# Recurrence channels in 11 tiles of five groups, and K's rope summed by VectorE

## The chip, the cores and the metric

One core of a Trainium2 chip runs the whole program. The metric is the device time of one execution in microseconds (us), here the median of three runs; a profiled execution stands beside them.

## The reference, cut to what matters

Two transformer blocks follow each other on x of 256 tokens by 1024 channels, all in fp32. The first has a gated linear recurrence over 1344 channels beside three forms of attention, and a feed-forward part. The second has attention with rope beside a gated mixing unit, and another feed-forward part. The change touches the recurrence of the first and the rope of the second.

```python
def rg_lru(x, w_a, b_a, w_x, b_x, lam):          # 16 blocks of 84 channels
    xb = x.reshape(bsz, s, RNN_BLOCKS, RNN_BLOCK_W)
    r = sigmoid(einsum('bsnc,ncd->bsnd', xb, w_a).reshape(...) + b_a)
    i = sigmoid(einsum('bsnc,ncd->bsnd', xb, w_x).reshape(...) + b_x)
    log_a = LRU_C * r * log_sigmoid(lam)
    a = exp(log_a)
    u = sqrt(-expm1(2.0 * log_a)) * (i * x)
    ...                                          # h[t] = a[t] * h[t-1] + u[t]
hr = rg_lru(causal_dwconv(rx, rnn_conv_w, rnn_conv_b), ...)
y_rnn = (hr * gelu(rgate)) @ w_rnn_out           # 1344 -> 1024

def rope(t, pos):                                # q and k of the second block
    rot = concatenate([-t2, t1], axis=-1)
    return t * cos + rot * sin
```

## The kernel before, in words

All weights come as one stream, cut into chunks of up to 128 x 2048 fp32 (1 MB), in the order of the list `chunk_list()`. For a split chunk ScalarE makes a rounded first part WH (L577), and VectorE the rest WL = RAW - WH (L965); TensorE multiplies both, three matmuls of 256 tokens for each 128 x 128 of weights (`f_tile`, L1576 to L1578) or of 512 columns (`t_part`, L1600 to L1602). Raw weights have two slots, split ones three. All waits are on semaphores, and the order on each engine is written out by hand: each engine runs one loop over the chunks c. TensorE does the scores of one attention unit (`unit_qk`, L1639 and L1643), the chunk's own matmuls (`main`), and `window`. ScalarE and VectorE do in it the split for chunk c + 2, their part of the unit, `side(c)` (what reads this chunk's result) and `window`.

The part around the change has 24 chunks, counted w = 0 to 23 from `W0`. The 1344 channels are 16 blocks of 84. Four blocks make a group of three tiles of 126 rows, so there are 12 tiles in four groups of equal size (RG = 3, NG = 4). A group is three rnn chunks (a tile of rx and of rgate each), an mg chunk (gates of the merge), the gate chunk ri and another mg chunk, so the gate chunks are w = 4, 10, 16 and 22. Tiles 0 and 1 of a group share the fourth block, half each. Its crossing parts are extra matmuls on 42 rows (L1859, L1861), added to the banks of tiles 0 and 1. Tile 2 has none. It is therefore computed and read first (`GATE_ORDER = (2, 0, 1)`), and its semaphore `ri_part` is counted at once:

```python
for m, t in enumerate(GATE_ORDER):          # ScalarE, side() of an ri chunk
    bank = wait_mb(eng, c, m)
    ...                                     # tanh to TR and TI, L729 and L730
    if m == 0 and i:
        rg_first(i - 1)
    if m == 0 and 0 <= c - W0 - 3 < NU:
        unit_exp(c - W0 - 3)
```

The rest of a group's work is placed by steps counted from its gate chunk: logarithm (`rg_log_a`) one chunk on, exponential and square in that chunk's `window`, a product on VectorE two on, square root and gelu (L650, L652, ScalarE) three on, the product with the input (`rg_input`) four on, the scan over the tokens with the product by the gelu (`rg_scan`, L1027 and L1029) five on, and the two parts for ro (`rg_first`, L603, and `rg_second`, L1033) six on, in the next gate chunk. The last group has its scan four and its parts five chunks on.

Sixteen attention units run beside this, one for each chunk from w = 3: scores on TensorE in banks 2 and 3, maximum (`unit_max`, L979) on VectorE, exponentials (`unit_exp`, L597, four) on ScalarE, weights (`unit_weights`, L991 to L997) on VectorE one chunk later, transposes (L1672) and sums (L1695) five and six. Units in which bit 1 of the number is set have 256 keys, the others 128. `unit_qk(u)` waits for `exp_done` of unit u - 1. After w = 23 come ao (4 chunks), ro (8, the product with w_rnn_out over the 12 tiles in AH and AL), wo, and the feed-forward part, which uses AH and AL as a ring of 12.

In the second block in2 chunks 1 and 3 give Q and K. VectorE makes two products in RT for each of two token tiles (L1274, L1278), and GpSimd adds them to RQK (L543). TensorE transposes Q's after in2 chunk 3 and K's after chunk 4 (L1787), and waits for the sums.

Of the kernel before, what the change touches and what calls it, by code (L numbers as in the profile page):

```python
# [27 lines left out]
P = 128  # L28
# [6 lines left out]
NR = 12  # L35
RB = D_RNN // 16
RG = 3
HB = RB // 2
NG = NR // RG
# [18 lines left out]
GATE_ORDER = (2, 0, 1)  # L58
GATE_COLS = RG * RP + HB


def rnn_rows():

    rows = -np.ones((RG, RP), int)
    rows[0, 0:64] = np.arange(64)
    rows[0, 64:64 + HB] = 3 * RB + np.arange(HB)
    rows[0, 64 + HB:RP] = np.arange(64, RB)
    rows[1, 0:HB] = 3 * RB + HB + np.arange(HB)
    rows[1, HB:RP] = RB + np.arange(RB)
    rows[2, 0:RB] = 2 * RB + np.arange(RB)  # L70
    return rows


def chunk_list():
# [63 lines left out]
_n = 0  # L138
# [14 lines left out]
RG_LOG_A, RG_A, RG_SQUARES, RG_ROOTS, RG_SCAN, RG_SPLIT = 4, 5, 6, 7, 8, 9  # L153
# [11 lines left out]
def rg_group(w, step):  # L165

    g, r = divmod(w - step, 2 * RG)
    return g if r == 0 and 0 <= g < NG else None


def psum_uses(kinds_by_reader):

    uses, counts, seen = [], [], {"act": 0, "dve": 0, "m": 0}
    for c, (kind, _, _, _) in enumerate(CHUNKS):
        if kind in kinds_by_reader:
            reader, n = kinds_by_reader[kind]
            for _ in range(n):
# [18 lines left out]
for _c, (_kind, _i, _, _) in enumerate(CHUNKS):  # L196
    if _kind in MB_READERS:
        MB_NO[_c] = _n
        _n += MB_READERS[_kind][1]


def two_block_program(nc, A_w, A_x, A_cols, A_consts, A_g1, A_g2, A_og, A_gln, A_ln1, A_ln2, A_ws, A_out):
    ctx = ExitStack()
    with ctx:
# [23 lines left out]
        AH = put("AH", [P, NR, TOK], F32R)  # L228
        AL = put("AL", [P, NR, TOK], F32R)
# [188 lines left out]
        def mb_of(m):  # L418

            return 2 if m == MB_NO[AT["mg", 2 * NG - 1]] else m % 2  # L420
# [86 lines left out]
        def _(eng):  # L507
# [53 lines left out]
        def _(eng):  # L561
# [39 lines left out]
            def rg_first(G):  # L601
                eng.wait_ge(scan_ready, G + 1)
                eng.activation(AH[0:RP, RG * G:RG * G + RG, :], XC[:, G % 2, :, :], ACT.Copy).then_inc(g_hi, 1)  # L603
# [14 lines left out]
            def window(w):  # L618
# [22 lines left out]
                if G is not None:  # L641
                    eng.wait_ge(la_ready, G + 1)
                    link(eng.activation(AA[:, :, :], TR[:, :, :], ACT.Exp))
                    eng.activation(TR[:, :, :], TR[:, :, :], ACT.Tanh)
                    eng.wait_ge(ix_ready, G + 1)
                    eng.activation(XC[:, G % 2, :, :], AA[:, :, :], ACT.Square).then_inc(sq_ready, 1)
                G = rg_group(w, RG_ROOTS)
                if G is not None:
                    eng.wait_ge(w_ready, G + 1)
                    eng.activation(XC[:, G % 2, :, :], TR[:, :, :], ACT.Sqrt, scale=-0.25).then_inc(root_ready, 1)  # L650
                    eng.wait_ge(rnn_g, RG * (G + 1))
                    eng.activation(RGT[:, G % 2, :, :], RGT[:, G % 2, :, :], ACT.Gelu_apprx_tanh)\  # L652
# [19 lines left out]
            def side(c):  # L672
# [36 lines left out]
                if kind == "rnn":  # L709
                    bank = wait_mb(eng, c)  # L710
                    G, t = divmod(i, RG)
# [11 lines left out]
                if kind == "ri":  # L723
                    if i >= 1:
                        eng.wait_ge(rnn_in, i)
                    for m, t in enumerate(GATE_ORDER):
                        bank = wait_mb(eng, c, m)
                        n = RG * i + t
# [160 lines left out]
            def up_first(i):  # L889
                eng.wait_ge(up_prod, i + 1)  # L890
                if i >= NR:
                    eng.wait_ge(chunk_done, AT["dn", (i - NR) // 2] + 1)
                eng.activation(AH[:, i % NR, :], CG[:, i % 4, 0, :], ACT.Copy).then_inc(up_hi, 1)
# [7 lines left out]
            def up2_first(i):  # L901
                eng.wait_ge(up2_prod, i + 1)
                if i >= NR:
                    eng.wait_ge(chunk_done, AT["dn2", (i - NR) // 2] + 1)
                eng.activation(AH[:, i % NR, :], SG[:, i % 4, :], ACT.Copy).then_inc(up2_hi, 1)
# [45 lines left out]
        def _(eng):  # L951
# [55 lines left out]
            def rg_log_a(G):  # L1007
                eng.wait_ge(mb_act, MB_COUNTS[MB_NO[AT["ri", G]] + RG - 1])
                if G == 0:
                    eng.wait_ge(c4_ready, 1)  # L1010
                eng.scalar_tensor_tensor(TR[:, :, :], TR[:, :, :], 1.0,
                                         c4[0:RP, RG * G:RG * G + RG].unsqueeze(2).broadcast_to([RP, RG, TOK]),
                                         ALU.add, ALU.mult).then_inc(la_ready, 1)
                eng.scalar_tensor_tensor(TI[:, :, :], TI[:, :, :], 1.0, XC[:, G % 2, :, :], ALU.add, ALU.mult)\
                   .then_inc(ix_ready, 1)

            def rg_input(G):
                x = XC[:, G % 2, :, :]
                eng.wait_ge(root_ready, 2 * G + 1)
                eng.tensor_tensor(x, x, TI[:, :, :], ALU.mult).then_inc(rnn_in, 1)  # L1020

            def rg_scan(G):
                x = XC[:, G % 2, :, :]
                eng.wait_ge(rnn_in, G + 1)
                eng.wait_ge(a_starts, G + 1)
                u, a = (b.rearrange("p k t -> p (k t)") for b in (x, AA[:, :, :]))
                link(eng.tensor_tensor_scan(u, a, u, 0.0, ALU.mult, ALU.add))  # L1027
                eng.wait_ge(root_ready, 2 * G + 2)
                eng.tensor_tensor(x, x, RGT[:, G % 2, :, :], ALU.mult).then_inc(scan_ready, 1)  # L1029

# [1229 lines left out]
```

## Time and profile before

| | |
|---|---|
| median of 3 runs | 853.76 us (853.51 to 854.21) |
| profiled execution | 856.47 us, its span 854.7 |
| TensorE matmuls | 840.2 us busy, 98% of the span |
| TensorE weight loads | 737.7 us, 86% |
| VectorE | 579.1 us, 68% |
| ScalarE | 492.7 us, 58% |
| GpSimd | 33.0 us, 4% |
| mean granted TensorE clock | 0.994 |
| HBM read | 143.82 MB, 169 GB/s over the span |

Times in the rows are microseconds from the start of the span, unless ns is written. PE is TensorE, PEld its weight loads, DVE is VectorE, ACT is ScalarE, POOL is GpSimd. L12 is line 12 of the kernel. A matmul's time runs to its modelled end and overlaps the next one's, so what one costs is the distance between starts.

### The profile page before, as it was taken

The page shows a single profiled execution, that of the slowest core. Times are in us where ns is not written, and L with a number is a line of the kernel's source. Part 1 is how long each engine was busy: PE and PEld are TensorE (multiplying, and loading weights), DVE is VectorE, ACT ScalarE, POOL GpSimd, SP SyncE. Part 2 cuts the span into 40 slices and gives each one's busy share as a digit, 9 for nine tenths or more (in the row PEclk, how much of TensorE's full clock was granted, in tenths as well). Part 3 has the DMA queues.
Part 4 walks back from the last instruction along what each step waited for, and adds up shares of the span by engine and source line. Part 5 has one row for each costly group of instructions (what it writes and reads, how often), then busy time and mean ns, then how long its engine had stood idle before and what let it go on. Part 6 is the DMA issues. An engine that isn't in the chain of part 4 may idle for free.

```text
span 854.7 us, 12695 instructions
## 1 busy us (share of the span) xinstructions
PE 840.2 (98%) x5225; PEld 737.7 (86%) x5225; DVE 579.1 (68%) x751; ACT 492.7 (58%) x730; POOL 33.0 (4%) x42
## 2 busy tenths in 40 slices
PE   8999999999999999999999999999999999999996
PEld 7999989798898998888888888887887888888884
DVE  5572578696865866698887787765777664564555
ACT  6463468787866544476665665545754654554542
POOL 0100200000000000000000000013110000000000
PEclk9999999999999999999999999999999999999999
DMA  8436425142334667245555556475345455556441
GB/s 320 155 119 234 161 73 193 50 147 78 139 119 143 207 224 287 101 154 196 193 198 197 186 171 212 144 287 185 121 148 197 148 201 192 171 182 230 156 148 49
DMA packets 22361, 145.68 MB, mean 170 GB/s; under 512 B 2592, under 2 KB 3104, under 8 KB 7968
## 3 DMA queue, kind: packets, MB, share of 16 engines
q1 hardware_dynamic: 20880, 139.56, 47.0%
q10 hardware_dynamic: 1424, 5.31, 1.7%
q8 instruction: 41, 0.67, 0.3%
q14 instruction: 16, 0.13, 0.0%
HBM read 143.82 MB, written 1.05 MB: 169 GB/s over the span
## 4 chain that ended last, share of the span: by engine, by line
PE 86%; DVE 6%; DMA 2%; issue 2%; ACT 2%; POOL 1%; SPq 0%; DVEq 0%; POOLq 0%; ACTq 0%
PE PS L1588 17%; PE PS L1591 9%; PE PS L1576 8%; PE PS L1577 8%; PE PS L1578 8%; PE PS L1600 8%; PE PS L1601 8%; PE PS L1602 8%; DMA RAW<-in_w_stream 2%; DVE WL L965 2%; PE PS L1639 2%; DVE CG L1387 2%; PE PS L1695 1%; PE PS L1672 1%; PE PS L1643 1%
## 5 line engine op out<-in xcount | busy, mean ns | idle before, releaser
L965 DVE TENSOR_TENSOR WL<-RAW,WH 128x2048 fp32r<-128x2048 f32 (+2 forms) x129 | 288.6, 2238 | 71.3 <-ACT WH L577 71.2
L577 ACT ACTIVATE WH<-RAW 128x2048 fp32r<-128x2048 f32 (+2 forms) x129 | 241.4, 1873 | 70.3 <-PE PS L1602 28.7
L1576 PE MATMUL PS<-BHL,WH 128*128 128x256 f32 (+2 forms) x424 | 121.3, 286 | 0.0
L1577 PE MATMUL PS<-BHL,WH 128*128 128x256 f32 (+2 forms) x424 | 120.1, 283 | 0.0
L1578 PE MATMUL PS<-BHL,WL 128*128 128x256 f32 (+2 forms) x424 | 120.1, 283 | 0.0
L1376 DVE TENSOR_TENSOR HLS<-PS,HLS 128x512 f32<-128x512 f32 x46 | 31.8, 692 | 102.9 <-ACT HLS L872 102.0
L1588 PE MATMUL PS<-CHL,WH 128*128 128x512 f32 x384 | 96.0, 392 | 0.3 <-DVE WL L965 0.3
L1588 PE MATMUL PS<-BHL,WH 128*128 128x512 f32 x352 | 87.9, 392 | 0.0
L1576 PEld LDWEIGHTS PS<-BHL,WH 128*128 128x128 f32 (+2 forms) x424 | 80.4, 190 | 1.9 <-issue 1.6
L1588 PEld LDWEIGHTS PS<-CHL,WH 128*128 128x128 f32 x384 | 69.6, 189 | 13.6 <-DVE WL L965 0.7
L1577 PEld LDWEIGHTS PS<-BHL,WH 128*128 128x128 f32 (+2 forms) x424 | 80.5, 190 | 0.0
L1578 PEld LDWEIGHTS PS<-BHL,WL 128*128 128x128 f32 (+2 forms) x424 | 80.3, 189 | 0.0
L872 ACT ACTIVATE HLS<-PS 128x512 f32<-128x512 f32 x46 | 27.2, 592 | 87.7 <-PE PS L1591 87.7
L1588 PEld LDWEIGHTS PS<-BHL,WH 128*128 128x128 f32 x352 | 63.9, 189 | 11.8
L1600 PE MATMUL PS<-WH,AH 128*128 128x512 f32 x184 | 72.2, 392 | 0.5 <-DVE WL L965 0.3
L1601 PE MATMUL PS<-WL,AH 128*128 128x512 f32 x184 | 71.8, 390 | 0.0
L1602 PE MATMUL PS<-WH,AL 128*128 128x512 f32 x184 | 71.6, 389 | 0.0
L1600 PE MATMUL PS<-WH,BHL 128*128 128x512 f32 x144 | 57.2, 398 | 0.6 <-DVE BHL L1497 0.6
L1601 PE MATMUL PS<-WL,BHL 128*128 128x512 f32 x144 | 56.5, 392 | 0.0
L1602 PE MATMUL PS<-WH,BHL 128*128 128x512 f32 x144 | 56.4, 392 | 0.0
L1591 PEld LDWEIGHTS PS<-CHL,WL 128*128 128x128 f32 x384 | 52.4, 190 | 3.7
L1591 PE MATMUL PS<-CHL,WL 128*128 128x256 f32 x384 | 53.5, 282 | 0.0
(278 smaller groups left out, 1391.9 us busy)
## 6 DMA issues: line engine op xcount, KB each, us to landing
RAW<-in_w_stream SPq DMA_DIRECT2D x108, 1024.0 KB, 4.9
RAW<-in_w_stream SPq DMA_DIRECT2D x12, 1008.0 KB, 5.1
RAW<-in_w_stream SPq DMA_DIRECT2D x8, 768.0 KB, 4.3
WF<-in_w_stream SPq DMA_DIRECT2D x2, 1024.0 KB, 5.4
LN<-in_ln ACTq DMA_DIRECT2D x2, 1024.0 KB, 7.1
WF<-in_w_stream SPq DMA_DIRECT2D x4, 420.0 KB, 3.2
X<-in_x SPq DMA_DIRECT2D x2, 512.0 KB, 4.1
RAW<-in_w_stream SPq DMA_DIRECT2D x2, 512.0 KB, 6.7
```

The source lines that it names most:

```text
L577: eng.activation(WH[:, c % NSLOT, 0:CHUNKS[c][2]], raw(c), ACT.Copy).then_inc(w_hi, 1)
L872: eng.activation(HLS[:, n % 4, :, :], PS[:, bank:bank + 2, TOK:2 * TOK], ACT.Copy).then_inc(half_copied, 1)
L965: eng.tensor_tensor(WL[:, c % NSLOT, 0:CHUNKS[c][2]], raw(c), f32(WH[:, c % NSLOT, 0:CHUNKS[c][2]]), ALU.subtract).then_inc(w_lo, 1)
L1376: eng.tensor_tensor(HLS[:, n % 4, :, :], PS[:, bank:bank + 2, 0:TOK], HLS[:, n % 4, :, :], ALU.add)\
L1576: eng.matmul(out, wh, H[0:parts, k, :], start=(k == 0), stop=False)
L1577: eng.matmul(out, wh, L[0:parts, k, :], start=False, stop=False)
L1578: last = eng.matmul(out, wl, H[0:parts, k, :], start=False, stop=(k == nk - 1))
L1588: eng.matmul(PS[:, bank, :], wh, HL[:, k, :, :].rearrange("p a t -> p (a t)"), start=(k == 0), stop=False)
L1591: last = eng.matmul(PS[:, bank, 0:TOK], wl, HL[:, k, 0, :], start=False, stop=(k == KD - 1))
L1600: eng.matmul(out, h, wh, start=(start and n == 0), stop=False)
L1601: eng.matmul(out, h, wl, start=False, stop=False)
L1602: last = eng.matmul(out, l, wh, start=False, stop=(stop and n == len(ks) - 1))
```

## The change

The channels are packed into 11 tiles: five groups of 2, 2, 3, 2 and 2 tiles, with 3, 3, 4, 3 and 3 blocks. The chunk list has 11 rnn, 8 mg and now 5 ri chunks, so this part still has 24 chunks; the gate chunks are w = 3, 7, 12, 17 and 22. The steps are found by kind of chunk (`rg_group`) and keep their distances from the gate chunk, but the scan now follows the input product at once, four chunks on: at the end of the chunk (`window`) where this is an mg chunk, and ahead of the chunk's other work where it is not (w = 7 and, as before, w = 26). A group of two tiles has the order (0, 1). ro multiplies 11 tiles. The ring of the feed-forward parts stays at 12 (NA). Q's rope sums stay on GpSimd, while K's are done by VectorE right behind its products.

```diff
-NR = 12
+NR = 11
+NA = 12
+RG_TILES = (2, 2, 3, 2, 2)
+RG_AT = tuple(sum(RG_TILES[:g]) for g in range(len(RG_TILES) + 1))
+RG_OF = [(g, t) for g, n in enumerate(RG_TILES) for t in range(n)]
+RG_FILL = (("mg", "ri"), ("mg", "ri"), ("mg", "ri", "mg"), ("mg", "ri", "mg"), ("mg", "ri", "mg"))
-NG = NR // RG
+NG = len(RG_TILES)
-GATE_ORDER = (2, 0, 1)
-GATE_COLS = RG * RP + HB
+def gate_order(g):
+    return (2, 0, 1)[3 - RG_TILES[g]:]
+def gate_cols(g):
+    return RG_TILES[g] * RP + HB
...
     for g in range(NG):
-        out += [("rnn", RG * g + t, 2 * KD * RP, True) for t in range(RG)]
-        out += [("mg", 2 * g, CHUNK, True), ("ri", g, 2 * GATE_COLS, False), ("mg", 2 * g + 1, CHUNK, True)]
+        out += [("rnn", RG_AT[g] + t, 2 * KD * RP, True) for t in range(RG_TILES[g])]
+        for kind in RG_FILL[g]:
+            out.append(("mg", mg, CHUNK, True) if kind == "mg" else ("ri", g, 2 * gate_cols(g), False))
+            mg += kind == "mg"
...
-RG_LOG_A, RG_A, RG_SQUARES, RG_ROOTS, RG_SCAN, RG_SPLIT = 4, 5, 6, 7, 8, 9
+RG_LOG_A, RG_A, RG_SQUARES, RG_ROOTS, RG_SCAN, RG_SPLIT = 0, 1, 2, 3, 4, 5
 def rg_group(w, step):
-    g, r = divmod(w - step, 2 * RG)
-    return g if r == 0 and 0 <= g < NG else None
+    kind, g, _, _ = CHUNKS[max(0, W0 + w - step)]
+    return g if kind == "ri" else None
...
         def wait_mb(eng, c, n=0):
-            if CHUNKS[c][0] == "ri" and n < RG - 1:
-                eng.wait_ge(ri_part, (RG - 1) * CHUNKS[c][1] + n + 1)
+            kind, i, _, _ = CHUNKS[c]
+            if kind == "ri" and n < RG_TILES[i] - 1:
+                eng.wait_ge(ri_part, RG_AT[i] - i + n + 1)
...
             # GpSimd
-            for i in range(4):
-                b, t = divmod(i, 2)
-                eng.wait_ge(rope_parts, i + 1)
-                eng.tensor_tensor(RQK[:, b, t, :], RT[:, i % 2, 0, :], RT[:, i % 2, 1, :], ALU.add).then_inc(roped, 1)
+            for t in range(NT):
+                eng.wait_ge(rope_parts, t + 1)
+                eng.tensor_tensor(RQK[:, 0, t, :], RT[:, t, 0, :], RT[:, t, 1, :], ALU.add).then_inc(roped, 1)
...
             # VectorE
             def rg_input_of(w):
                 G = rg_group(w, RG_SCAN)
-                if G is not None and G < NG - 1:
+                if G is not None and CHUNKS[W0 + w][0] == "mg":
                     rg_input(G)
+                    rg_scan(G)
...
                             if j >= 2:
-                                eng.wait_ge(roped, j - 1)
+                                eng.wait_ge(roped, j)
...
-                            ins.then_inc(rope_parts, 1)
+                            if b == 0:
+                                ins.then_inc(rope_parts, 1)
+                            else:
+                                link(ins)
+                                eng.tensor_tensor(RQK[:, 1, t, :], RT[:, t, 0, :], RT[:, t, 1, :], ALU.add).then_inc(roped, 1)
...
-                if rg_group(c - W0, RG_SCAN) == NG - 1:
-                    rg_input(NG - 1)
-                    rg_scan(NG - 1)
+                G = rg_group(c - W0, RG_SCAN)
+                if G is not None and CHUNKS[c][0] != "mg":
+                    rg_input(G)
+                    rg_scan(G)
...
                 G = rg_group(c - W0, RG_SPLIT)
-                if G is not None and G < NG - 1:
-                    rg_scan(G)
                 if G == NG - 1:
                     rg_second(G)
```

All operations of a group take `0:n` of their tiles, n being the group's number of tiles, and the host lays out channels, gate weights and w_rnn_out for the new tiles.

## Rows read from the trace of the kernel before

**Rows 1.** The page: chain that ended last, share of the span by engine
```profile
PE 86%; DVE 6%; DMA 2%; issue 2%; ACT 2%; POOL 1%; SPq 0%; DVEq 0%; POOLq 0%; ACTq 0%
```
**Rows 2.** TensorE's waits: who waited for whom, total us, times, longest us
```profile
PE PS L1787 <- POOL RQK L543: 2.0, 1, 2.0
```
**Rows 3.** TensorE's timeline: start us, us; an rnn chunk to the next one
```profile
188.37 0.28 PE L1576 MATMUL PS<-BHL,WH 128*126 128x256 f32 x1
...
194.04 0.60 PE L1672 MATMUL PS<-CN,SMC 128*128 128x128 f32 x4
...
197.00 0.28 PE L1576 MATMUL PS<-BHL,WH 128*126 128x256 f32 x1
```
**Rows 4.** VectorE's timeline: first reader of two ro chunks
```profile
310.87 0.42 DVE L1207 SCALAR_TENSOR_TENSOR MG<-MG,PS 128x256 f32<-128x256 f32 x1 [0.98 <-PE PS L1578]
...
315.19 0.42 DVE L1207 SCALAR_TENSOR_TENSOR MG<-MG,PS 128x256 f32<-128x256 f32 x1 [0.98 <-PE PS L1578]
```
**Rows 5.** TensorE's timeline: the first gate chunk and what follows
```profile
115.56 3.08 PE L1851 MATMUL PS<-XC,WF 126*126 126x256 f32 x12
118.57 0.41 PE L1859 MATMUL PS<-XC,WF 42*42 42x256 f32 x1
...
119.57 0.66 PE L1734 MATMUL PS<-CN,SC 128*128 128x128 f32 x4
```
**Rows 6.** DMA issues: gate weights, KB each, us to landing
```profile
WF<-in_w_stream SPq DMA_DIRECT2D x4, 420.0 KB, 3.2
```
**Rows 7.** Timelines of VectorE and GpSimd at K's rope
```profile
582.35 0.68 DVE L1274 TENSOR_TENSOR RT<-PS,CN 128x512 f32<-128x512 f32 x1
...
585.03 3.31 POOL L543 TENSOR_TENSOR RQK<-RT 128x512 f32<-128x512 f32 x1
```
**Rows 8.** TensorE's timeline at K's transposes
```profile
586.17 0.27 PE L1787 MATMUL PS<-CN,RQK 128*128 128x128 f32 x1
```
**Rows 9.** Stretch: us, busy PE, PEld, DVE, ACT, POOL, granted clock, DMA, GB/s
```profile
588.33:591.74 3.41, 3.34 (x12) 2.96 (x13) 0.00 (x0) 1.60 (x2) 1.06 (x2) 0.52 0.80 296
```
**Rows 10.** Timelines of three engines in the second gate chunk
```profile
163.90 3.15 PE L1851 MATMUL PS<-XC,WF 126*126 126x256 f32 x12
...
165.02 0.47 ACT L729 ACTIVATE TR<-PS,hba 126x256 f32<-126x256 f32 x1 [2.03 <-PE PS L1851]
...
165.75 0.84 ACT L603 ACTIVATE AH<-XC 126x768 fp32r<-126x768 f32 x1
165.84 1.23 DVE L997 TENSOR_TENSOR SM<-SM,wt 128x1024 f32<-128x1024 f32 x1
...
167.97 0.33 PE L1672 MATMUL PS<-CN,SMC 128*128 128x128 f32 x1
...
168.66 0.49 ACT L729 ACTIVATE TR<-PS,hba 126x256 f32<-126x256 f32 x1
...
169.58 0.71 PE L1639 MATMUL PS<-KT,QT 64*128 64x128 f32 x8
```
**Rows 11.** The same view of a stretch, behind the narrow matmuls of w = 2
```profile
107.00:110.50 3.50, 3.50 (x18) 3.50 (x19) 3.29 (x8) 0.63 (x1) 0.00 (x0) 0.53 0.00 0
```
**Rows 12.** Groups of VectorE by line and shape: busy us, mean ns
```profile
L1027 DVE TENSOR_TENSOR_SCAN XC<-AA,XC 126x768 f32<-126x768 f32 x4 | 7.0, 1752 | 0.0
...
L1310 DVE TENSOR_TENSOR ZT<-ZT,GLN 128x512 f32<-128x512 f32 x2 | 1.4, 692 | 0.1
```
**Rows 13.** ScalarE's timeline: gelu, then a table load ahead of the exponentials
```profile
199.56 0.85 ACT L652 ACTIVATE RGT<-RGT 126x768 f32<-126x768 f32 x1
200.42 1.28 ACT L597 ACT_TABLE_LOAD   x1
201.72 0.57 ACT L597 ACTIVATE SMC<-PS,nb,rq 128x256 f32<-128x256 f32 x1
```
**Rows 14.** Timelines of TensorE and VectorE behind the last gate chunk
```profile
264.11 0.39 PE L1576 MATMUL PS<-BHL,WH 128*128 128x256 f32 x1
...
267.62 2.29 DVE L965 TENSOR_TENSOR WL<-RAW,WH 128x2048 fp32r<-128x2048 f32 x1 [3.88 <-ACT WH L577]
```

More of the change, by code:

```diff
@@ L56, with rnn_rows @@
 NSLOT = 3
-GATE_ORDER = (2, 0, 1)
-GATE_COLS = RG * RP + HB
-def rnn_rows():
-    rows = -np.ones((RG, RP), int)
+def gate_order(g):
+    return (2, 0, 1)[3 - RG_TILES[g]:]
+def gate_cols(g):
+    return RG_TILES[g] * RP + HB
+def rnn_rows(g):
+    n = RG_TILES[g]
+    first = RB * (RG_AT[g] + g)
+    rows = -np.ones((n, RP), int)
     rows[0, 0:64] = np.arange(64)
-    rows[0, 64:64 + HB] = 3 * RB + np.arange(HB)
+    rows[0, 64:64 + HB] = n * RB + np.arange(HB)
     rows[0, 64 + HB:RP] = np.arange(64, RB)
-    rows[1, 0:HB] = 3 * RB + HB + np.arange(HB)
+    rows[1, 0:HB] = n * RB + HB + np.arange(HB)
     rows[1, HB:RP] = RB + np.arange(RB)
-    rows[2, 0:RB] = 2 * RB + np.arange(RB)
-    return rows
+    if n == 3:
+        rows[2, 0:RB] = 2 * RB + np.arange(RB)
+    return np.where(rows >= 0, rows + first, -1)
 def chunk_list():
@@ L165, in rg_group @@
 def rg_group(w, step):
-    g, r = divmod(w - step, 2 * RG)
-    return g if r == 0 and 0 <= g < NG else None
+    kind, g, _, _ = CHUNKS[max(0, W0 + w - step)]
+    return g if kind == "ri" else None
 def psum_uses(kinds_by_reader):
     uses, counts, seen = [], [], {"act": 0, "dve": 0, "m": 0}
-    for c, (kind, _, _, _) in enumerate(CHUNKS):
+    for c, (kind, i, _, _) in enumerate(CHUNKS):
         if kind in kinds_by_reader:
             reader, n = kinds_by_reader[kind]
-            for _ in range(n):
+            for _ in range(RG_TILES[i] if kind == "ri" else n):
                 seen[reader] += 1
@@ L227, in two_block_program @@
         a_at = top[0]
-        AH = put("AH", [P, NR, TOK], F32R)
-        AL = put("AL", [P, NR, TOK], F32R)
+        AH = put("AH", [P, NA, TOK], F32R)
+        AL = put("AL", [P, NA, TOK], F32R)
         BHL = put("BHL", [P, KD, 2, TOK], F32R)
@@ L602, in rg_first @@
                 eng.wait_ge(scan_ready, G + 1)
-                eng.activation(AH[0:RP, RG * G:RG * G + RG, :], XC[:, G % 2, :, :], ACT.Copy).then_inc(g_hi, 1)
+                eng.activation(AH[0:RP, RG_AT[G]:RG_AT[G + 1], :], XC[:, G % 2, 0:RG_TILES[G], :], ACT.Copy).then_inc(g_hi, 1)
             def unit_pt(u):
@@ L710, in side @@
                     bank = wait_mb(eng, c)
-                    G, t = divmod(i, RG)
+                    G, t = RG_OF[i]
                     if G >= 2:
@@ L890, in up_first @@
                 eng.wait_ge(up_prod, i + 1)
-                if i >= NR:
-                    eng.wait_ge(chunk_done, AT["dn", (i - NR) // 2] + 1)
-                eng.activation(AH[:, i % NR, :], CG[:, i % 4, 0, :], ACT.Copy).then_inc(up_hi, 1)
+                if i >= NA:
+                    eng.wait_ge(chunk_done, AT["dn", (i - NA) // 2] + 1)
+                eng.activation(AH[:, i % NA, :], CG[:, i % 4, 0, :], ACT.Copy).then_inc(up_hi, 1)
             def up2_silu_of(i):
@@ L902, in up2_first @@
                 eng.wait_ge(up2_prod, i + 1)
-                if i >= NR:
-                    eng.wait_ge(chunk_done, AT["dn2", (i - NR) // 2] + 1)
-                eng.activation(AH[:, i % NR, :], SG[:, i % 4, :], ACT.Copy).then_inc(up2_hi, 1)
+                if i >= NA:
+                    eng.wait_ge(chunk_done, AT["dn2", (i - NA) // 2] + 1)
+                eng.activation(AH[:, i % NA, :], SG[:, i % 4, :], ACT.Copy).then_inc(up2_hi, 1)
             def gained_hi(kp):
@@ L1857, in main @@
                         cols = slice(256 * which, 256 * which + 256)
-                        other = w[:, which, RG * RP:RG * RP + HB]
+                        other = w[:, which, RP * RG_TILES[i]:gate_cols(i)]
                         ins = eng.matmul(PS[64:64 + HB, banks[0], cols], other[0:HB], XC[0:HB, i % 2, 1, :],
@@ L1908, in down_half @@
                         return t_part(PS[:, first_bank + 2 * t + n, :], cc, 512,
-                                      [((2 * j + k) % NR, 1024 * k + 512 * n) for k in range(2)], AH, AL, t,
+                                      [((2 * j + k) % NA, 1024 * k + 512 * n) for k in range(2)], AH, AL, t,
                                       j == 0, j == n_all - 1)
@@ L1939, in main @@
                     if i == 6:
[L1940 removed]
+                        eng.wait_ge(roped, 4)
                     if i == 8:
@@ L2122, in tile @@
         return w[:, width * m:width * m + width]
-    rows_of = rnn_rows()
     def spread(w, axis):
-        span = RG * RB * 4 // 3
         w = np.moveaxis(w, axis, 0)
@@ L2131, in spread @@
         for i in range(NR):
-            g, t = divmod(i, RG)
-            used = rows_of[t] >= 0
-            out[i, used] = w[span * g + rows_of[t][used]]
+            g, t = RG_OF[i]
+            rows_of = rnn_rows(g)[t]
+            used = rows_of >= 0
+            out[i, used] = w[rows_of[used]]
         return out
@@ L2140, in gates_blocks @@
     def gates_blocks(g):
-        out = np.zeros((P, 2, GATE_COLS), np.float32)
+        n = RG_TILES[g]
+        rows_of = rnn_rows(g)
+        out = np.zeros((P, 2, gate_cols(g)), np.float32)
         for which, w in enumerate((a["rg_w_a"], a["rg_w_x"])):
-            dense = np.zeros((4 * RB, 4 * RB), np.float32)
-            for b in range(4):
-                dense[RB * b:RB * b + RB, RB * b:RB * b + RB] = w[4 * g + b]
-            for t in range(RG):
+            dense = np.zeros((D_RNN, D_RNN), np.float32)
+            for b in range(16):
+                dense[RB * b:RB * b + RB, RB * b:RB * b + RB] = w[b]
+            for t in range(n):
                 used = np.nonzero(rows_of[t] >= 0)[0]
@@ L2151, in gates_blocks @@
             first, second = rows_of[0, 64:64 + HB], rows_of[1, 0:HB]
-            out[0:HB, which, RG * RP:] = dense[second[:, None], first[None, :]]
-            out[64:64 + HB, which, RG * RP:] = dense[first[:, None], second[None, :]]
+            out[0:HB, which, n * RP:] = dense[second[:, None], first[None, :]]
+            out[64:64 + HB, which, n * RP:] = dense[first[:, None], second[None, :]]
         return out.reshape(P, -1)
```

66 lines of the change are left out of this document (36 added, 30 removed).

## The prediction

> **What bounds the kernel now.** I read the chain that ended last first: TensorE holds 86% of it [rows 1], and the page has it busy for 98% of the span. The list of TensorE's waits adds only a few us, the largest of them 2.0 us for GpSimd's rope sum [rows 2]. So what leaves TensorE leaves the time, and what makes it wait is added to the time. VectorE (68% busy) and ScalarE (58%) are hidden only as long as each piece that TensorE needs is there before TensorE asks for it. So the last view is the timeline of the three engines around the four gate chunks, where I asked of each piece how early it is today.
>
> **One channel tile less.** An rnn chunk is 48 matmuls; from its first to the next operation it takes 194.04 - 188.37 = 5.67 us [rows 3]. In ro each of the 8 chunks loses 3 of its 36 matmuls. Two ro ends lie 4.32 us apart [rows 4], so a matmul there is 0.12 us and 24 of them are 2.9 us. What VectorE and ScalarE lose (a split, three taps, smaller copies) lies beside TensorE's work and brings nothing of its own. The ro pace becomes 3.96 us, and neither of the two has more than some 3 us of work in it, so I take the 2.9 whole.
>
> **Gates.** The gate chunk of today takes 119.57 - 115.56 = 4.0 us; 12 passes over three tiles are 118.57 - 115.56 = 3.0 of it [rows 5], so a tile is 1.0 and the crossing blocks are 1.0. After the change there is one chunk of 4.0 and four of 3.0: 16.0, as 4 x 4.0 today, so nothing. Their weights come in five loads of 294 or 420 KB in place of four of 420. On SP's queue each keeps its place behind the load of the chunk that follows the gates, and is free to go about two chunks (14 us) before its use; a landing takes 3.2 us [rows 6]: hidden.
>
> **K's rope.** VectorE starts on the parts of K's two token tiles at 582.35 and has them near 585.0, four operations each with the last two overlapping; GpSimd's adds end at 585.03 + 3.31 = 588.34 [rows 7]. TensorE asks at 586.17 [rows 8], waits, and then runs 3.41 us at a granted clock of 0.52 (the level of 1.2 GHz) [rows 9]. With both adds on VectorE (512 columns, 0.69 us each [rows 12], some 0.1 for each link) the second ends near 586.45. The wait shrinks by 588.34 - 586.45 = 1.9 us and, being 0.3 then, should cost no clock: 3.41 x 0.48 = 1.6 more. Gain 3.5 us. The split queued behind the adds on VectorE slips by 1.5 us, but it is for the chunk after next, which TensorE reaches some 7 us later. Bounds of this gain: 1.9 (the clock falls anyway) and 3.8 (no wait at all).
>
> Gains together: 5.7 + 2.9 + 3.5 = 12.1 us.
>
> **What the new groups put on the path.** TensorE can't start the scores of unit u+1 before ScalarE's exponentials of unit u, since both use one pair of banks. In a gate chunk ScalarE does these exponentials after the first tile's tanhs and after rg_first (the previous group's copy for ro). Today the first tile is tile 2, which has no crossing block: its tanh comes 165.02 - 163.90 = 1.1 us after the first gate matmul, and the exponentials are over by 168.66, 0.9 us before TensorE's next scores at 169.58 [rows 10]. In a group of two tiles the first is tile 0, whose semaphore is counted behind the crossing blocks: 4.1 us after the first gate matmul today, 3.1 with a tile less. From there: 0.73 for the tanhs (165.75 - 165.02), 0.84 for rg_first of three tiles and about 0.6 of two, 2.2 for four exponentials of 256 keys and 1.9 of 128 [rows 10]. TensorE is through with two tiles 3.0 after their start and with the transposes and sums behind them 1.6 later (169.58 - 167.97).
> Gates of group 0 (chunk 3 of this part, unit 0). They now stand where the mg chunk stood, right behind 32 narrow matmuls and in a stretch at 0.53 of the clock that ends near 110.5 [rows 11]. Some seven of eight passes run at half rate, so the crossing blocks end near 111.8, the tanhs at 112.6, the exponentials at 114.5. There is nothing between for TensorE: it waits 2.7 us. Today the mg chunk lies over this.
> Group 1 (chunk 7, unit 4), counted from the first gate matmul. VectorE's maximum and weights end at 2.6 (165.84 + 1.23 - 163.90 = 3.2 today, less 0.54 for a maximum of half the size). Then come, new in this chunk, the input product 0.69, the scan 1.2 (two thirds of 1.75) and the output product 0.69 [rows 12], done at 5.2. rg_first waits for that: 5.9. A square root and a gelu ended just before, and after them the exponential needs a table load of 1.28 [rows 13]: 7.2, and 9.15 with the exponentials. TensorE is there at 4.6, so it waits 4.6 us.
> The Trainium skill (ScalarE: Activation LUTs, "What ACT_TABLE_LOAD costs") counts a drain of 1.38 us on top of the load. In the trace the next activation starts 0.02 us behind the load [rows 13], so the trace does not agree; by the page this wait would be 6.0.
> Group 2 has three tiles and goes as today. Group 3 (chunk 17, unit 14): 3.1 + 0.73 + 0.84 + 2.3 = 7.0 against 4.6, a wait of 2.5 with the rounding. Group 4 has no unit any more.
> The two mg chunks 11 and 16 follow the chunk with root and gelu, and ScalarE has a split in them ahead of the exponentials, which no such chunk has today. From the end of the chunk before: copies 1.7, load, root, load, gelu 3.8, split 1.9, load 1.3, exponentials 1.95, together 10.7 (11.5 in chunk 16 with three tiles). TensorE asks 8.3 to 8.6 (one chunk, 197.00 - 188.37 [rows 3]) plus 1.6 later, at 9.9 and with the larger units of chunk 16 at 10.9: waits of 0.8 and 0.65. VectorE has input, scan and product of these groups at the end of the same chunks. The maxima behind them come 2 to 3 us late, but the exponentials that want them are later still, behind rg_first.
> Ahead of ao 0: the split of its weights stands behind the last gates on ScalarE and VectorE and ends at 269.91 today, when TensorE is ready (264.11 + 5.76) [rows 14]. TensorE will be there 1.0 earlier, the split 0.4: a wait of 0.65.
> Waits together: 2.7 + 4.6 + 2.5 + 0.8 + 0.65 + 0.65 = 11.9 us. Bounds: 8.3 (2.7, 3.1 if the scan were over in time, 2.5) and 15 (each of the small ones doubled, 1 us more at group 1).
>
> **Clock.** At the rope a wait of 2.0 us was followed by 3.4 us at 0.52 [rows 2, 9]. I expect the like behind 2.7, 4.6 and 2.5 us, in part over time in which TensorE waits anyway, in part not falling at the third: 1.3 + 1.7 + 0.9 = 3.9. Bounds: 0 and 8 (two such stretches behind each of the first two and one behind the third).
>
> Sum: -12.1 + 11.9 + 3.9 = +3.7 us. The profiled execution took 856.47 (its span is 854.7), so the same view would have 860.2 after; the median of the runs shown is 853.76, 2.7 lower than the profiled one, and with the same +3.7 gives **857.5**.
>
> **Rivals.**
> A. The exponentials stay hidden and the whole gain comes: 853.76 - 12.1 = 841.7. For it speaks that they are hidden by 0.9 us today; against it the order in the code, which costs more than 0.9.
> B. Not slower. VectorE's scan is over before group 1's tanhs, so only 2.7 + 3.1 + 2.5 = 8.3 us are waited at the gates, nothing elsewhere, and the clock stays up: -3.8, 850.0. It decides whether rg_first of group 1 finds the scan done, that is whether VectorE is through 1.3 us sooner than I count. Against it: maximum, weights and scan stand in one chunk, in this order.
> C. The waits come as worked out, but the clock holds: -0.2, 853.6. For it: no gate chunk of today was followed by a lower clock.
> D. The clock falls twice behind the longer waits, 4 us more: 861.5.
> That the change does not do what it says (12 rnn chunks, GpSimd still adding K's parts) would leave 853.8; the diff excludes it.
>
> **How the numbers follow.** Chances: the forecast 0.43 (its own range 855.5 to 860), A 0.08, B 0.15, C 0.22, D 0.12. The range from 848.5 to 861.5 leaves out A, B's lower tail and half of D. Over 0.2% is 1.7 us, about what a measurement of this kernel can tell from no change: below 852.1 or above 855.5. Faster is A, most of B and a tail of C, 0.24; the same is the rest of C and the fringes of B and of the forecast, 0.20; slower is the rest of the forecast, D and the upper tail of C, 0.56.
>
> **What would show it.** In the list of TensorE's waits the score matmuls wait for ScalarE's exponentials three times, the longest near 4.6 us; behind them the granted clock is near 0.5; the rope wait is gone; ro ends lie 3.96 us apart. I am wrong if TensorE goes from the gates to the next scores without a gap, or if its new waits lie on ro or on splits other than ao 0's.

## The result, and the profile after

| | before | changed |
|---|---|---|
| first set, median | 853.63 us (853.42 to 854.21, 4 runs) | 859.88 us (858.24 to 862.18, 4 runs) |
| ratio, 95% interval | | 1.0055 (1.003 to 1.008) |
| second set, median | 853.80 us (23 runs) | 861.09 us (856.96 to 861.95, 6 runs) |
| ratio, 95% interval | | 1.0065 (1.0043 to 1.0088) |
| profiled execution | 856.47 us, span 854.7, clock 0.994 | 862.18 us, span 860.4, clock 0.987 |

The change makes the kernel slower by 0.55 to 0.65%, 4.7 to 5.5 us. The forecast was +3.7 (857.5). The difference of the profiled executions is 5.7. One of the 23 executions of the kernel before took 2921 us; the ratio and the clocks below leave it out.

Executions of one kernel differ, in part by their granted clock: the four of the changed kernel took 862.18, 858.24, 858.45 and 861.31 us at mean clocks of 0.987, 0.993, 0.992 and 0.987. This matters below: the median of the kernel before over 22 executions is 0.997, and the one of its profile had 0.994. 0.003 of 855 us is 2.6 us, about what separates that profile (856.47) from the median. The clock is not all of it: the kernel before took 852.01 to 855.91 us in the seven of these 22 executions that have 0.997.

The view to open first is again the chain, beside [rows 1]. TensorE's share falls from 86 to 81% and ScalarE's grows from 2 to 5%:

```profile
PE 81%; DVE 7%; ACT 5%; issue 3%; DMA 2%; POOL 0%; SPq 0%; DVEq 0%; POOLq 0%; ACTq 0%
```

So TensorE now waits, and mostly for ScalarE. Its list of waits answers to [rows 2] (who waited for whom, total us, times, longest):

```profile
PE PS L1666 <- ACT SM L614: 7.9, 3, 4.6
...
PE PS L1666 <- ACT SMC L614: 2.8, 2, 2.3
...
PE PS L1814 <- DVE RQK L1308: 1.0, 1, 1.0
```

L1666 is the first matmul of a unit's scores, L614 the exponentials of the unit before. TensorE's timeline shows the five one by one (start, us; the wait ahead of it in brackets):

```profile
114.82 1.22 PE L1666 MATMUL PS<-KT,QT 64*128 64x128 f32 x8 [2.68 <-ACT SM L614]
...
151.21 0.75 PE L1666 MATMUL PS<-KT,QT 64*128 64x128 f32 x8 [4.63 <-ACT SM L614]
...
187.96 0.71 PE L1666 MATMUL PS<-KT,QT 64*128 64x128 f32 x8 [0.53 <-ACT SMC L614]
...
231.08 1.13 PE L1666 MATMUL PS<-KT,QT 64*128 64x256 f32 x8 [0.61 <-ACT SM L614]
...
239.27 0.92 PE L1666 MATMUL PS<-KT,QT 64*128 64x256 f32 x6 [2.30 <-ACT SMC L614]
```

The first, second and last follow the gates of groups 0, 1 and 3; the other two follow mg chunks 11 and 16. The longest has this history on ScalarE and VectorE, counted from the gates' start at 142.08:

```profile
145.36 0.47 ACT L748 ACTIVATE TR<-PS,hba 126x256 f32<-126x256 f32 x1 [0.65 <-DVE XC L1041]
...
146.62 0.69 DVE L1051 TENSOR_TENSOR XC<-XC,RGT 126x512 f32<-126x512 f32 x1
147.34 0.63 ACT L620 ACTIVATE AH<-XC 126x512 fp32r<-126x512 f32 x1 [1.14 <-DVE XC L1051]
147.99 1.28 ACT L614 ACT_TABLE_LOAD   x1
149.28 0.46 ACT L614 ACTIVATE SM<-PS,nb,rq 128x128 f32<-128x128 f32 x1
```

Tanhs, then 1.14 us for VectorE's product behind the scan, the copy, the table load, and only then the exponentials: each piece is short, and they stand in one line. The load is followed by the exponential 0.01 us later, as in [rows 13].

The stretches at half clock are the third view (busy PE, PEld, DVE, ACT, POOL, clock, DMA, GB/s):

```profile
107.50:110.90 3.40, 3.40 (x10) 2.59 (x9) 3.19 (x9) 0.63 (x1) 0.00 (x0) 0.52 0.00 0
114.30:121.20 6.90, 6.38 (x33) 6.16 (x34) 4.29 (x7) 6.53 (x15) 0.00 (x0) 0.51 0.10 13
151.90:155.30 3.40, 3.40 (x18) 3.40 (x17) 0.85 (x2) 3.40 (x4) 0.00 (x0) 0.52 0.00 0
240.60:244.00 3.40, 3.40 (x18) 3.40 (x18) 1.49 (x2) 3.40 (x4) 0.00 (x0) 0.51 0.03 5
...
595.80:599.20 3.40, 3.40 (x19) 2.96 (x20) 2.11 (x1) 2.41 (x2) 0.00 (x0) 1.00 0.24 31
```

The first was there before [rows 11]. Three more, the first of them twice as long, stand at the three gate waits, and the last line shows the time behind the rope's wait at full clock, where [rows 9] had 0.52.

Last, two places where the gain is seen. Ro ends lie 3.96 us apart, against 4.32 in [rows 4], and TensorE passes ro in 31.68 us against 34.63 (first ro matmul to first wo matmul):

```profile
308.63 0.42 DVE L1231 SCALAR_TENSOR_TENSOR MG<-MG,PS 128x256 f32<-128x256 f32 x1 [0.86 <-PE PS L1605]
...
312.59 0.42 DVE L1231 SCALAR_TENSOR_TENSOR MG<-MG,PS 128x256 f32<-128x256 f32 x1 [0.86 <-PE PS L1605]
```

At K's rope, which answers to [rows 7, 8], VectorE starts 3.0 us ahead of TensorE's first transpose of K (591.46 and 594.48), where it was 3.8 us before (582.35 and 586.17), since the split ahead of it (589.25) waited for its weights:

```profile
589.25 2.29 DVE L984 TENSOR_TENSOR WL<-RAW,WH 128x2048 fp32r<-128x2048 f32 x1 [3.35 <-ACT WH L594]
...
591.46 0.68 DVE L1298 TENSOR_TENSOR RT<-PS,CN 128x512 f32<-128x512 f32 x1
...
595.02 0.69 DVE L1308 TENSOR_TENSOR RQK<-RT 128x512 f32<-128x512 f32 x1
...
595.77 0.98 PE L1814 MATMUL PS<-CN,RQK 128*128 128x128 f32 x7 [1.02 <-DVE RQK L1308]
```

### The profile page after: what moved, and what is told of

Read it like the earlier page. It is cut to its first block, busy times and chain, and to the rows that moved or that the text cites. A ratio compares the mean times of both kernels' runs of the same rounds, so it can differ in the third digit from the quotient of the medians.

```text
span 860.4 us, 12569 instructions
## 1 busy us (share of the span) xinstructions
PE 835.7 (97%) x5157; PEld 732.7 (85%) x5157; DVE 574.4 (67%) x757; ACT 492.1 (57%) x734; POOL 28.4 (3%) x40
## 4 chain that ended last, share of the span: by engine, by line
PE 81%; DVE 7%; ACT 5%; issue 3%; DMA 2%; POOL 0%; SPq 0%; DVEq 0%; POOLq 0%; ACTq 0%
PE PS L1615 17%; PE PS L1618 9%; PE PS L1627 8%; PE PS L1628 8%; PE PS L1629 8%; PE PS L1603 7%; PE PS L1604 7%; PE PS L1605 7%; DMA RAW<-in_w_stream 2%; DVE WL L984 2%; PE PS L1666 2%; DVE CG L1415 2%; ACT WH L594 1%; PE PS L1722 1%; PE PS L1670 1%
## 5 line engine op out<-in xcount | busy, mean ns | idle before, releaser
L984 DVE TENSOR_TENSOR WL<-RAW,WH 128x2048 fp32r<-128x2048 f32 (+2 forms) x128 | 285.2, 2228 | 74.0 <-ACT WH L594 73.9
L594 ACT ACTIVATE WH<-RAW 128x2048 fp32r<-128x2048 f32 (+2 forms) x128 | 238.6, 1867 | 71.2 <-DMA RAW<-in_w_stream 30.0
L1603 PE MATMUL PS<-BHL,WH 128*128 128x256 f32 (+2 forms) x408 | 118.3, 290 | 0.0
L1604 PE MATMUL PS<-BHL,WH 128*128 128x256 f32 (+2 forms) x408 | 117.1, 287 | 0.0
L1605 PE MATMUL PS<-BHL,WL 128*128 128x256 f32 (+2 forms) x408 | 117.0, 287 | 0.0
L1603 PEld LDWEIGHTS PS<-BHL,WH 128*128 128x128 f32 (+2 forms) x408 | 79.2, 194 | 1.9 <-issue 1.6
L1604 PEld LDWEIGHTS PS<-BHL,WH 128*128 128x128 f32 (+2 forms) x408 | 79.0, 194 | 0.0
```

The source lines that it names most:

```text
L594: eng.activation(WH[:, c % NSLOT, 0:CHUNKS[c][2]], raw(c), ACT.Copy).then_inc(w_hi, 1)
L984: eng.tensor_tensor(WL[:, c % NSLOT, 0:CHUNKS[c][2]], raw(c), f32(WH[:, c % NSLOT, 0:CHUNKS[c][2]]), ALU.subtract).then_inc(w_lo, 1)
L1603: eng.matmul(out, wh, H[0:parts, k, :], start=(k == 0), stop=False)
L1604: eng.matmul(out, wh, L[0:parts, k, :], start=False, stop=False)
L1605: last = eng.matmul(out, wl, H[0:parts, k, :], start=False, stop=(k == nk - 1))
```

## Experiments

Each ratio is to the kernel before on the same chip. A median is of its own kernel alone; where medians and ratios differ I go by the ratios, times 853.8 us. after_again, tiles_only, rope_only and exp_first ran on one chip, fill_waits, copy_late, first_two and order_all on a second, fill_group0 and order_more on a third; differences of ratios across them assume that the ratio does not depend on the chip.

**The changed kernel again** (after_again), unedited.

> The changed kernel as it is, beside the next three on one chip. Theory: its times fall near two values, about 858.3 and 861.7 us, as the four taken so far (858.24, 858.45, 861.31, 862.18, at mean granted clocks of 0.993, 0.992, 0.987 and 0.987), because one execution in two has one or two stretches more at half clock behind the new waits: 3.4 us more of the slower pair's span. The median over before is then 1.003 to 1.009. Rival: the two values belong to the two chips or days of the runs; then all of one call are near one of them.

Measured: 1.0065 (1.0043 to 1.0088); 861.62, 860.59, 859.07, 856.96, 861.95 and 861.59 us at clocks of 0.987, 0.991, 0.991, 0.994, 0.988 and 0.987. The times are spread rather than in two groups, as the theory had it, but nearly in order of the clock, on one chip. The rival (a matter of the chip) is out, and of the theory only the clock is left. The profile of this execution has the same gate waits and its half-clock stretches at the same four places.

**The parts apart** (tiles_only, rope_only).

```diff
 # tiles_only, against the changed kernel       (rope_only: the reverse, against the kernel before)
-            for t in range(NT):
-                eng.wait_ge(rope_parts, t + 1)
-                eng.tensor_tensor(RQK[:, 0, t, :], RT[:, t, 0, :], RT[:, t, 1, :], ALU.add).then_inc(roped, 1)
+            for i in range(4):
+                b, t = divmod(i, 2)
+                eng.wait_ge(rope_parts, i + 1)
+                eng.tensor_tensor(RQK[:, b, t, :], RT[:, i % 2, 0, :], RT[:, i % 2, 1, :], ALU.add).then_inc(roped, 1)
...
-                                eng.wait_ge(roped, j)
+                                eng.wait_ge(roped, j - 1)
...
-                            if b == 0:
-                                ins.then_inc(rope_parts, 1)
-                            else:
-                                link(ins)
-                                eng.tensor_tensor(RQK[:, 1, t, :], RT[:, t, 0, :], RT[:, t, 1, :], ALU.add).then_inc(roped, 1)
+                            ins.then_inc(rope_parts, 1)
...
-                        eng.wait_ge(roped, 4)
+                        eng.wait_ge(rope_parts, 4)
```

> The eleven tiles without the rope's edit: GpSimd adds K's parts again. Theory: the two parts of the change add up. The rope's edit gained 2.6 us between the two profiles (the changed kernel reaches K's part 8.3 us late and leaves it 5.7 late), so this kernel is 2.6 us slower than the changed one, some 8 us over before, with a wait of about 2.0 us for GpSimd's sum and 3.4 us at half clock behind it. Rival: the rope's wait is not on the path (another wait takes its place) and the time is that of the changed kernel.

> The kernel before with the rope's edit alone: VectorE adds both of K's parts. Theory: 2.6 to 3.5 us faster than before (wait 2.0 down to 0.3 or 1.0, and 1.6 us of lost clock back), so about 850 to 851. Rival one: the clock falls behind a wait of 1 us as well, and only 1.0 to 1.6 us come. Rival two: nothing, since the next wait takes its place.

Measured: tiles_only 1.0099 (1.0076 to 1.0123), 862.83 us; rope_only 0.9985 (0.9969 to 1.0), 853.51 us. tiles_only is 8.5 us over before, as expected (some 8). The rope's edit is worth 1.3 us alone and 2.9 beside the tiles (1.0099 less 1.0065). Neither is clear of noise: the interval of rope_only reaches 1.0 and its medians differ by 0.3 us, and the other two intervals overlap. rope_only missed its range (850 to 851); its number is that of rival one, but no fall of the clock stands behind its wait in the profile. In rope_only its wait fell to 0.3 us, as predicted:

```profile
PE PS L1790 <- DVE RQK L1283: 0.3, 1, 0.3
```

So the wait goes as worked out, and with it 1.7 us in the profile. The 1.3 measured is less, at a lower clock: the twelve executions of rope_only have a median of 0.995, the kernel before 0.997, and the one in the profile, at 0.998, took 851.4. Where the others lost clock no trace shows; this stays open.

The prediction looked only at the second of K's two adds on GpSimd, 3.31 us [rows 7]. The first took 1.30 us in the same trace. The second runs beside a split on VectorE, from 584.87 to 587.22:

```profile
583.77 1.30 POOL L543 TENSOR_TENSOR RQK<-RT 128x512 f32<-128x512 f32 x1 [4.51 <-DVE RT L1278]
...
584.87 2.35 DVE L965 TENSOR_TENSOR WL<-RAW,WH 128x2048 fp32r<-128x2048 f32 x1
```

All five such pairs in the traces of before, tiles_only and the changed kernel are alike (1.3 and 3.3 us), and the 2.0 us more are about TensorE's wait. So the split on VectorE may have made the wait, and moving the split might have removed it with the add left on GpSimd. No run tests this.

The clock's part at the rope, 1.6 us in the prediction, was read from one profiled execution. In tiles_only TensorE waited longer there than in the kernel before (first fence below), and no half-clock stretch followed: the three of its profile before the end are all at the gates (second fence below).

```profile
PE PS L1811 <- POOL RQK L561: 2.6, 1, 2.6
```
```profile
114.80:118.20 3.40, 3.40 (x18) 3.40 (x17) 2.92 (x5) 3.40 (x6) 0.00 (x0) 0.50 0.00 0
148.90:152.30 3.40, 3.40 (x19) 3.23 (x18) 0.65 (x2) 3.40 (x5) 0.00 (x0) 0.51 0.00 0
237.60:241.00 3.40, 3.40 (x17) 3.40 (x17) 1.29 (x2) 3.40 (x4) 0.00 (x0) 0.51 0.02 5
```

**Exponentials first** (exp_first, then first_two).

```diff
 # exp_first: ScalarE, in front of side(c)
-                if 0 <= c - W0 - 3 < NU and CHUNKS[c][0] != "ri":
+                if 0 <= c - W0 - 3 < NU:
                     unit_exp(c - W0 - 3)
...
-                        if m == 0 and 0 <= c - W0 - 3 < NU:
-                            unit_exp(c - W0 - 3)
 # first_two: the same, but not where RG_TILES[i] == 3
```

> The changed kernel with ScalarE's exponentials ahead of the first tile's tanhs and of the copy for ro in every gate chunk; nothing else. Theory: the order of the code on ScalarE makes the three gate waits. They fall from 2.7, 4.6 and 2.3 us to about 0.7 (VectorE's maximum of unit 0 ends at 110.9), 1.3 (table load 1.28 and four exponentials 1.8 from the gelu's end) and 0, together 7.6 less, and the half-clock stretches behind them go, 3 to 6 us more: 847 to 850 us, faster than before. Rival: the tanhs, now later, hold up the bank of the next tile or the logarithms, and new waits of the same size stand in the next chunks: 855 to 860. A second rival: waits go, the clock falls all the same: about 852.5.

Measured: 1.0046 (1.003 to 1.0061), 857.86 us. The gate waits fell, at group 1 from 4.63 to 1.36 as expected, at group 3 from 2.30 to 1.16 where 0 was expected. The time is the first rival's, 855 to 860, by its mechanism: the bank of the next tile is held up. It happens in one chunk only:

```profile
187.73 1.93 PE L1876 MATMUL PS<-XC,WF 126*126 126x256 f32 x4 [4.84 <-ACT TI L749]
```

In the chunk of three tiles, tile 0 needs the bank of tile 2, so TensorE waits for tile 2's tanhs, which now stood behind exponentials that themselves waited 3.87 us for VectorE's maximum. The clock fell behind it (187.9 to 191.3 at 0.50).

> As the kernel with the exponentials first, but only in the gate chunks of two tiles; the chunk with three tiles keeps its order (tile 2's tanhs, copy, exponentials). Theory: the wait of 4.8 us that stood for the tanh of tile 2 in the three-tile chunk, and the half-clock stretch behind it (187.9 us), came from there alone; both go, 5 to 6.5 us below the 857.9 of that kernel: 851.5 to 853. Rival: the group of three waits for something else (VectorE's maximum, behind its scan), and the wait only moves: 856 to 858.

Measured: 0.9972 (0.996 to 0.9984), 850.81 us: faster than before, and 0.7 us under the expected range. Against exp_first 1.0046 less 0.9972 is 6.3 us, the wait of 4.84 and a stretch of 3.4 us at half clock. The rival (only moved) is out. Of the waits for exponentials 5.1 us are left, 3.5 of them at the gates (0.98, 1.37 and 1.16) in place of 9.6:

```profile
PE PS L1666 <- ACT SM L614: 3.2, 4, 1.4
...
PE PS L1666 <- ACT SMC L614: 1.9, 3, 1.2
```

Against the changed kernel, the order of two calls on ScalarE is worth 1.0065 - 0.9972, 7.9 us.

**The copy for ro behind the exponentials** (copy_late).

```diff
-                        if m == 0 and i:
-                            rg_first(i - 1)
                         if m == 0 and 0 <= c - W0 - 3 < NU:
                             unit_exp(c - W0 - 3)
+                        if m == 0 and i:
+                            rg_first(i - 1)
```

> The changed kernel with the copy for ro (rg_first) behind the exponentials in the gate chunks, nothing else. Theory: VectorE's scan and the copy behind it stand before the exponentials of group 1 (1.14 us waited for the product and 0.63 of copy) and 0.86 of copy before those of group 3: the waits fall from 4.6 to 2.8 and from 2.3 to 1.5 us, 2.6 us less, and 857 to 858 if the clock falls as before. Rival: the table load alone sets them (it starts with the gelu's end) and nothing changes.

Measured: 1.0021 (1.0006 to 1.0035), 856.04 us. The waits for exponentials sum to 8.2 us (6.1 and 2.1), 2.5 less than 10.7, as expected: the scan was on the path, by way of the copy. The time fell by 3.8 (1.0065 less 1.0021), more than that, to 1 us under the expected range. This profile has no half-clock stretch behind groups 1 and 3, though at group 1 TensorE still waited 2.86 us:

```profile
149.25 0.72 PE L1666 MATMUL PS<-KT,QT 64*128 64x128 f32 x8 [2.86 <-ACT SM L614]
```

**Work for nothing in the waits** (fill_waits, fill_group0). The extra matmuls write a bank that the next chunk overwrites; no output depends on them.

```diff
+FILLER = {0: 18, 1: 34, 3: 16}                # fill_group0: {0: 18}
...
             for c in range(NCH):
+                if c and CHUNKS[c - 1][0] == "ri" and CHUNKS[c - 1][1] in FILLER:
+                    bank = mb_bank(MB_NO[c])
+                    for n in range(FILLER[CHUNKS[c - 1][1]]):
+                        eng.matmul(PS[0:RP, bank, 0:256], BH[:, n % KD, 0:RP], BH[:, n % KD, :], start=True, stop=True)
                 if 0 <= c - W0 - 3 < NU:
                     unit_qk(c - W0 - 3)
```

> The changed kernel with work for nothing in its gate waits: behind the gates of groups 0, 1 and 3 TensorE does 18, 34 and 16 more matmuls of 256 columns into the bank that the next chunk overwrites, 2.2, 4.1 and 1.9 us that fit into waits of 2.7, 4.6 and 2.3. Theory: the waits' length alone is 9.6 us of the loss, the lost clock behind them is the rest; with TensorE kept busy the stretches at half clock near 114, 152 and 240 us go, and with them 4 to 6.5 us: 854 to 857, mean clock 0.995 or more. Rival: the clock falls for another reason (the narrow matmuls of the crossing blocks and of the scores), the stretches stay, and the time is the changed kernel's, 860, or more.

> The changed kernel with the 18 matmuls for nothing behind the gates of group 0 alone. Filling all three waits brought 5.5 us (860.5, the mean of the changed kernel's two medians, to 855.0). Theory: the 6.8 us at half clock near 114 us, behind group 0's wait, were 3.1 us of it, the two stretches behind groups 1 and 3 the rest: 857 to 858. Rival: the loss at group 0 belongs to the narrow matmuls ahead of its gates and not to the wait: then filling there brings 1.5 us or less, 859 or more.

Measured: fill_waits 1.0014 (1.0003 to 1.0026), 855.0 us; fill_group0 1.004 (1.0024 to 1.0056), 857.88 us. With the gaps filled, the profile of fill_waits has no stretch at half clock at the gates (same columns as above):

```profile
107.50:110.90 3.40, 2.88 (x18) 1.72 (x16) 3.19 (x9) 0.81 (x2) 0.00 (x0) 1.00 0.00 0
...
114.30:121.20 6.90, 6.90 (x62) 6.61 (x60) 6.09 (x9) 5.49 (x12) 0.00 (x0) 1.00 0.33 96
...
152.00:155.40 3.40, 3.40 (x32) 3.39 (x30) 3.33 (x5) 3.23 (x12) 0.00 (x0) 1.00 0.30 39
```

The first line stands ahead of the first extra matmul (111.50), so its full clock is no work of theirs.

Six of the twelve executions of fill_waits have a clock of 0.998 and none is below 0.995, while the changed kernel's second set had 0.987 to 0.994. TensorE gets to the next scores no earlier by this, so the 4.4 us (1.0065 less 1.0014; 5 to 6 by the medians) are put down to the clock alone. (At group 0 it gets there some 0.5 us later: the extra matmuls waited for their bank and ended behind the exponentials. So the clock's share is a little more.) About half of it, 2.1 us by the ratios and 2.6 to 3.2 by the medians, is group 0's; the intervals of fill_group0 and of the changed kernel overlap. In the profile of fill_group0 group 0's stretch is gone and the one at group 1 is twice as long as in the changed kernel, so the stretches are not independent of each other or differ by execution:

```profile
145.40:152.30 6.90, 4.83 (x25) 4.60 (x26) 1.71 (x5) 6.89 (x15) 0.00 (x0) 0.51 0.00 0
```

The rival, narrow matmuls as the cause, is weakened and not excluded: the stretch at 107.5 stands ahead of the first wait and comes in some executions of most kernels here.

**The order mended** (order_all, then order_more). Beside first_two: on ScalarE the copy for ro last in the gate chunk and the gelu one chunk ahead of the root; on VectorE unit 0's maximum ahead of the compressed scores, and the scan behind the next chunk's maximum and weights. order_more moves ao 0's split ahead of the last tanhs.

```diff
 # ScalarE, window(w): at step RG_SQUARES, was with the root at RG_ROOTS
+                    eng.activation(RGT[:, G % 2, 0:n, :], RGT[:, G % 2, 0:n, :], ACT.Gelu_apprx_tanh)\
+                       .then_inc(root_ready, 1)
 # VectorE
                 if G is not None and CHUNKS[W0 + w][0] == "mg":
                     rg_input(G)
-                    rg_scan(G)
...
+                G = rg_group(c - W0 - 1, RG_SCAN)          # behind unit_max and unit_weights
+                if G is not None and CHUNKS[c - 1][0] == "mg":
+                    rg_scan(G)
 # order_more, ScalarE
+                if CHUNKS[c][:2] == ("ri", NG - 1):
+                    split(c + 2)
                 side(c)
```

> The changed kernel with the order of the code mended at each wait that the trace names: exponentials first in gate chunks of two tiles, the copy for ro last, the gelu a chunk ahead of the root, the maximum of unit 0 ahead of VectorE's compressed scores, and VectorE's scan of groups 1 to 3 behind the next chunk's maximum and weights. Theory: the tiles' 8.6 us and the rope's 1 to 2.6 come through when nothing waits at the gates: 843.5 to 846.5, mean clock 0.995 or more. Rival: ScalarE and VectorE are too full in these chunks for it, and the extra table loads bring waits of 2 us and more elsewhere: 848 to 853.

> As order_all (848.0), with the split of ao 0's weights ahead of the last gates' tanhs on ScalarE and in the gate chunk itself on VectorE. Theory: the wait of 0.41 us at ao 0 goes and nothing else moves: 847.6. Rival: the gates of the last group are held up behind the split and the tail of the group (logarithm, root, scan, copy) comes late for ro: 848 to 850. No difference from 848.0 that five rounds could tell is expected by either for the first.

Measured: order_all 0.993 (0.9918 to 0.9943), 848.04 us; order_more 0.9918 (0.9898 to 0.9938), 847.41 us. order_all missed its range by 1.5 us: three waits of 0.9, 0.45 and 0.23 us for exponentials are left, and its profiled execution has 6.8 us at half clock at group 0's gates with no wait beside them. The gain over the kernel before is 6 to 7 us, where the removed matmuls (5.7 and 2.95) and the rope's shorter wait (1.3) are 9.9. The three waits are 1.6 us of the difference; the rest is not accounted for. In order_more the wait at ao 0 is gone, and one of 0.36 us for a tanh is new at 113.59. It is in the range of the theory, but 0.6 us is less than these runs can tell from nothing.

## Why the prediction was right, and where its terms were off

The direction and the mechanism were right: the exponentials behind each two-tile gate chunk are late, and this costs more than the tile brings. The worked times of group 1 hold to 0.1 us: rg_first done at 5.9 (147.97 - 142.08 = 5.89), the table load at 7.2 (7.19).

| term | predicted | trace or runs |
|---|---|---|
| ro | -2.9 | -2.95 |
| rnn chunk less | -5.7 | about -5.6, worked out below |
| K's rope | -3.5 | -1.3 alone, -2.9 beside the tiles (ratios); wait 2.0 to 1.0 |
| wait, group 0 | 2.7 | 2.68 |
| wait, group 1 | 4.6 | 4.63 |
| wait, group 3 | 2.5 | 2.30 |
| mg 11, mg 16, ao 0 | 0.8, 0.65, 0.65 | 0.53, 0.61, 0.41 |
| clock | 3.9 | 4.4 (ratios), 5 to 6 (medians) |
| sum | +3.7 | +4.7, +5.5 (ratios), +5.7 (profiles) |

The chunk that is gone can be read from where ro starts, in the kernel before and in fill_waits:

```profile
293.32 0.36 PE L1576 MATMUL PS<-AH,WH 126*128 126x256 f32 x1
...
297.72 0.28 PE L1604 MATMUL PS<-AH,WH 126*128 126x256 f32 x1
```

fill_waits is there 4.4 us later. The kernel before had lost 1.7 us at half clock near 107 us, which fill_waits had not, so at equal clock it is 6.1. The waits, filled or not, are 11.2 us and 0.5 for the late extra matmuls, together 11.7, and 6.1 less 11.7 is -5.6.

Without the clock, and with 1.0 to 1.3 for the rope, -5.7 - 2.95 + 11.16 less that is +1.2 to +1.5 us; fill_waits, which has the waits and not the lost clock, measured +1.2. Rival C (waits, but the clock holds) is what that kernel is, and the changed kernel is not. Rival A fell at once. Rival B's premise was false: VectorE was not through sooner, rg_first waited 1.14 us for it. Copy_late, which takes it off the path, stays 0.2% above before.

Two terms were mis-sized. **K's rope**: the step "being 0.3 then, should cost no clock: 1.6 more" counted a stretch of the profiled execution as if every execution had it. The profile's clock is 0.994 where the median is 0.997, and only 7 of the 59 other executions of the experiments' three sets have 0.994 or less; how often this one stretch comes no run shows. The 2.7 us between the two times were named in the prediction, but it did not ask what they are made of. With the edit alone the gain was 1.3 us, not 3.5. And in the changed kernel the wait was 1.0, not 0.3, in the profile, since the split ahead of the rope started late (0.7 us). It was 0.6 in the second profile of the same kernel. **The clock**, by 0.5 to 2 us, which is why the total came out above the forecast: behind group 0 the text foresaw 1.3 us, where 6.8 us at half clock came, the second of the two stretches that rival D had. Group 3's, taken at 0.9, was 1.65. By size the outcome lies between the forecast and D, which also wanted group 1's doubled; that one stayed single in both profiles of the changed kernel and was doubled in fill_group0's. The waits, 0.75 too high, took a part of this back.

The drain of 1.38 us on top of a table load that the Trainium skill states (ScalarE: Activation LUTs, "What ACT_TABLE_LOAD costs") is not seen here either: with it the wait at group 1 would be 6.0, and it was 4.63.

## What to carry to other kernels

Before an edit takes work from the bound engine, list what the other engines must have done at that point and in which order they do it: here a gate chunk that was 1 us shorter on TensorE, and whose first tile came 2 us later, met a line of tanh, copy, table load and exponentials that nobody had shortened, and the order of two calls decided between +0.65% and -0.28%. When several calls stand in line on a side engine, put first what the bound engine asks for first, and look at each place of the loop apart: the same move was wrong in the chunk of three tiles. When a side engine looks slow, compare the same operation elsewhere in the trace: GpSimd's add took 1.30 us in one place and 3.31 in another. A stretch at half clock in one profile is no term of a sum until the mean clocks of the other executions say how often it comes.

## What the runs showed of the hardware

The clock fell to half behind waits of TensorE of 4.84, 4.63, 2.68 and 2.30 us (and 2.0 in the kernel before [rows 2, 9]), and not behind 2.86 (copy_late, group 1) or 2.6 us (tiles_only, rope). A wait of 2.88 us at group 0 of tiles_only was followed by such a stretch, so the length of a wait does not decide alone. Each of these stretches was 3.4 or 6.8 us and in part began only when TensorE was at work again: at group 1 it started some 0.5 us after the scores. Others came with no wait beside them, near 107 us in most kernels. Matmuls for nothing in the gaps kept the clock at 1.00 in the profiled execution and cost no time of their own where they ended before the wait did (groups 1 and 3, where 0.44 and 0.21 us were still waited).

GpSimd's add of 128x512 took 1.30 us, and 3.31 us beside a VectorE operation on two SBUF operands of 128x2048 (2.35 us); that the one holds up the other is not tested.
